# Two-block attention kernel: which steps stand beside which in the two attention stages

## What is computed

```
first block:  proj = norm(x) @ w_in
  8 heads of neighbourhood attention (qa, ka, va; mask and bias, head size 64)
  12 heads of dilated attention in 3 groups, dilation 1, 4, 16 (qb, kb rotated, vb)
  merged = gate_a * (o_a @ w_proj_a) + gate_b * (o_b @ w_proj_b);  x += gt1 * (merged @ w_o)
  x += gt2 * ffn(norm(x))
second block: joint attention over 512 tokens and 256 context tokens
  16 query heads in 8 pairs, 4 key heads; q, k normed per head, the 512 tokens' rotated
  x += gt1 * (o @ w_o);  x += gt2 * ffn(...), both for x and the context
  then a recurrent mixer in the place of attention, an ffn, and a last norm
```

## Time and profile before

| | us |
|---|---|
| median of 3 runs | 2740.07 |
| profiled execution | 2743.5 |
| its span, first to last instruction | 2741.7 |
| TensorE busy in the span | 2611.6 (95%) |
| VectorE, ScalarE, GpSimd busy | 1555.4, 1097.7, 1002.0 |

### The profile page before, as it was taken

How to read it: one execution, slowest core, us unless ns; L and a number is a source line. 1 busy time by engine, 2 the same in 40 slices (tenths; PEclk the granted TensorE clock), 3 DMA queues, 4 the chain that set the end, 5 groups by cost and what they waited for, 6 DMA issues and landing times. The chain is left out here.

```text
span 2741.7 us, 39030 instructions
## 1 busy us (share of the span) xinstructions
PE 2611.6 (95%) x15062; PEld 2181.7 (80%) x15062; DVE 1555.4 (57%) x2406; ACT 1097.7 (40%) x2040; POOL 1002.0 (37%) x571
## 2 busy tenths in 40 slices
PE   7997999999999999998999999999899998899998
PEld 5765778888888777777888888888788887788887
DVE  5554241787776256566755556655768777622224
ACT  4553442522324455556311211235555555522222
POOL 4344634556554312223332333341222112444444
PEclk9998999999999999999999999999999999999999
DMA  8643222354453100011333333411111111123222
GB/s 305 229 146 121 74 88 93 121 180 162 160 164 106 31 17 28 20 40 37 139 108 123 131 108 108 138 55 54 39 55 55 62 47 39 63 93 100 94 99 77
DMA packets 81463, 267.80 MB, mean 98 GB/s; under 512 B 8704, under 2 KB 16512, under 8 KB 81280
## 3 DMA queue, kind: packets, MB, share of 16 engines
q1 hardware_dynamic: 78944, 259.68, 28.2%
q10 hardware_dynamic: 2048, 4.33, 0.5%
q0 software_dynamic: 288, 1.31, 0.1%
HBM read 260.57 MB, written 4.72 MB: 97 GB/s over the span
## 5 line engine op out<-in xcount | busy, mean ns | idle before, releaser
L2261 POOL TENSOR_TENSOR SLO<-RAW,SHI 128x1024 fp32r<-128x1024 f32 (+1 forms) x290 | 716.5, 2473 | 1038.4 <-ACT SHI L2091 1038.4
L2091 ACT ACTIVATE SHI<-RAW 128x1024 fp32r<-128x1024 f32 (+1 forms) x334 | 345.1, 1037 | 949.6 <-PE PS L2526 947.8
L2524 PE MATMUL PS<-HLh,SHI 128*128 128x512 f32 (+1 forms) x1800 | 703.3, 391 | 7.6 <-DVE HLl L2330 4.7
L2526 PE MATMUL PS<-HLh,SLO 128*128 128x512 f32 (+1 forms) x1800 | 678.7, 377 | 0.0
L2525 PE MATMUL PS<-HLl,SHI 128*128 128x512 f32 (+1 forms) x1800 | 678.6, 377 | 0.0
L2524 PEld LDWEIGHTS PS<-HLh,SHI 128*128 128x128 f32 x1800 | 340.8, 189 | 79.8 <-issue 19.5
L2526 PEld LDWEIGHTS PS<-HLh,SLO 128*128 128x128 f32 x1800 | 340.2, 189 | 63.4
L2525 PEld LDWEIGHTS PS<-HLl,SHI 128*128 128x128 f32 x1800 | 341.1, 190 | 61.2 <-issue 6.3
L2524 PE MATMUL PS<-hh,SHI 128*128 128x512 f32 (+1 forms) x1024 | 363.1, 355 | 1.2 <-POOL hl L2280 1.2
L2526 PE MATMUL PS<-hh,SLO 128*128 128x512 f32 (+1 forms) x1024 | 356.4, 348 | 0.0
L2525 PE MATMUL PS<-hl,SHI 128*128 128x512 f32 (+1 forms) x1024 | 354.9, 347 | 0.0
(11 more groups left out here) (261 smaller groups left out, 3933.1 us busy)
## 6 DMA issues: line engine op xcount, KB each, us to landing
RAW<-in_k_w SPq DMA_DIRECT2D x318, 512.0 KB, 3.5
ADA<-in_k_w SPq DMA_DIRECT2D x132, 512.0 KB, 4.2
early<-in_k_w SPq DMA_DIRECT2D x12, 512.0 KB, 15.1
RAW<-in_k_w SPq DMA_DIRECT2D x16, 256.0 KB, 2.6
XL<-in_xT SPq DMA_DIRECT2D x4, 512.0 KB, 8.0
bi<-in_k_bias SPq DMA_DIRECT2D x16, 128.0 KB, 4.8
out<-XL SPq DMA_DIRECT2D x16, 128.0 KB, 1.8
bi<-in_k_bias SPq DMA_DIRECT2D x8, 192.0 KB, 3.9
```

The source lines that it names most:

```text
L2091: eng.activation(u.hi, u.w, ACT.Copy).then_inc(S["a_hi"], 1)
L2261: eng.tensor_tensor(u.lo, u.w, u.hi.bitcast(F32), ALU.subtract).then_inc(S["g_lo"], 1)
L2524: eng.matmul(st.out, lh, rh, start=st.first and j == 0, stop=False)
L2526: i = eng.matmul(st.out, ll, rh, start=False, stop=st.last and j == n - 1)
```

## The change

It has three edits.

1. `pipelined` has a switch, `shared`, that both stages set. A job without steps of its own no longer runs the tail before it; the tail is kept for the next job with steps. While a job waits, a "pause" is yielded ahead of each step of the tail, so that the attention sequence is asked for a step in between.
2. `weave` and `bgz` take "pause" as they take "wait".
3. Three empty pairs stand in `heads` between the 16 pairs of neighbourhood attention and the 8 dilated ones. A round whose pair is empty has no scores, flips or products for it.

```diff
@@ weave
-            known = len(emitted)
+            known, paused = len(emitted), False
             for p in sorted(left, key=lambda q: q[2]):
                 before = work[0]
                 got = next(p[0], "end")
-                if got == "wait":
+                if got in ("wait", "pause"):
                     p[3] = True
+                    paused |= got == "pause"
                     continue
@@ pipelined
-    def pipelined(jobs):
+    def pipelined(jobs, shared=False):
         tail = iter(())
         for job in jobs:
+            steps = 0
             while True:
...
                 if got == "wait":
+                    if shared:
+                        yield "pause"
                     yield next(tail, "wait")
                 else:
+                    steps += 1
                     next(tail, None)
                     yield
-            yield from tail
-            tail = new
+            if steps or not shared:
+                yield from tail
+                tail = new
         yield from tail
@@ attention
-            turn, read = 0 <= i - 2 < n, 0 <= i - 3 < n
+            turn, read = (0 <= k < n and pairs[k][0] is not None for k in (i - 2, i - 3))
...
-            if i < n:
+            if i < n and pairs[i][0] is not None:
@@ heads of the first stage
         heads += marked(na_items(j), [f"q {j}", f"k {j}"], f"na {j}")
+    heads += [None] * 6
@@ both weaves
-    weave((attention(heads, W, first_out), 0.6), (bgz(pipelined(dense)), 1.0))
+    weave((attention(heads, W, first_out), 0.6), (bgz(pipelined(dense, True)), 1.0))
-    weave((attention(heads, W, make2), 1.25), (pipelined(dense), 1.0))
+    weave((attention(heads, W, make2), 1.25), (pipelined(dense, True), 1.0))
```

More of the change, by code:

```diff
@@ L446, in weave @@
             else:
-                assert len(emitted) > known, "every sequence waits for another"
+                assert paused or len(emitted) > known, "every sequence waits for another"
     def run(gen):
```

## The result

The changed kernel takes 2753.04 us in the median of five runs (2751.29 to 2755.39). Beside it the kernel before took 2740.34 us (2739.62 to 2743.74). The ratio is 1.0045, 95% interval 1.0034 to 1.0056: slower by 12.7 us, where 15.5 less were forecast. The time lies outside the range as well.

The account below looks back on a forecast made before the run. PE was taken as the bound, busy 95% of the span, so time could come only from its idle time or clock. Terms -5.5 - 13.3 - 1.5 + 4.8 = -15.5 took 2740.07 to 2724.6 us, range 2711 to 2737.

Parts of the forecast that it names:

- the second stage, tiles 1 to 6: Query tiles' kept tails hold two PSUM banks during m0 to m2: +0.8 us a tile (-1.3 to +2.5), +4.8 in all.
- The walk through the banks: Second-stage tile, m0 to norms: new waits of 0.9, 0.3, 0.6 and 0.3, 2.1 us; 0.60 and 0.3 go.
- the low end of the range, 2711: Whole kernel: 2711 us, described as the sum with the best ends of passage and tiles.
- The third rival: m0 to m2 of six second-stage tiles: slower by PSUM banks, turning at 3.4 us more per tile, 2747 us; chance 0.13.
- First stage up to 217 us: Tails go beside the next job's chunks, removing norm waits of 0.69 and waits for VectorE: gain 5.5 us (4 to 5.8).
- The passage: Passage to dilated attention, 217 to 256 us: costs 8.5 instead of 21.8 us, a gain of 13.3 (9 to 19).
- The hole: First dilated scores wait for the rotated key from POOL, about 5.5 us (1.4 to 7), clock fall behind it 3.
- the second rival: Passage: Ada's VectorE step or a late unit delays the hole to 9 us, time 2733 or 2736; chance 0.12.
- The start of the second stage: First 30 us: the pause ends the rotation's wait, the second scores wait about 1.3 longer; gain 1.5 us (0 to 5).
- The forecast is wrong if the second stage changes its length by over 6 us: Sign in the profile after: a second-stage length change over 6 us would show the forecast wrong.

Follow-up runs that it names:

- e1: The changed kernel with the switch taken from the second stage, first stage as changed; 2726.7 us, ratio 0.9943 to the kernel before.
- e4: The changed kernel, but in the second stage both head norms run at once and only rotation and empty steps are kept; 2727.7 us, ratio 0.9948.
- e3: The changed kernel, but in the second stage VectorE copies a query tile's two PSUM banks to SBUF and the late norms read the copy; 2744.7 us.
- e11: The changed kernel, but second-stage query tiles' head norms run at once and only the giving back of their two banks stays late; 2741.6 us.

## Why the prediction was wrong

**The step that failed: the second stage, tiles 1 to 6.** It was priced at +0.8 us a tile, +4.8 in all, with +2.5 a tile as its upper end. The second norm of a tile comes every 44.2 us before and every 47.8 after (five periods each). These are the first and the last of the six, before and after:

```profile
987.41 0.67 PE L2532 MATMUL PS<-f,CONST 128*128 128x256 f32 x2 [0.83 <-ACT r L2118]
...
1208.47 0.67 PE L2532 MATMUL PS<-f,CONST 128*128 128x256 f32 x2 [0.60 <-DVE o L2388]
```

```profile
983.67 1.05 PE L2539 MATMUL PS<-f,CONST 128*128 128x256 f32 x2
...
1222.60 1.05 PE L2539 MATMUL PS<-f,CONST 128*128 128x256 f32 x2
```

That is (1222.60 - 983.67) - (1208.47 - 987.41) = 17.9 us in five periods, 3.6 a tile. The walk through the banks had the right order, and the two larger of its four waits came: m0's 0.9 as 0.7 for `o`, the norm's 0.6 as 0.58 for `XL`; the two of 0.3 did not, and all of the old 0.42 and 0.26 went. It stopped at the norms, where the banks come free. It left out m2's context chunk, whose bank is the flip's: 2.29 us in each of six tiles, for which the forecast has no term. But the step that moves is not only a holder of banks, it is also four instructions in three queues: a matmul, 0.69 + 0.63 us on ACT and 0.75 on VectorE. Before, it stood ahead of the reductions too, but early enough to be done in time; now VectorE's part ends 0.57 us too late for them, and the flip's copy is late by as much. On PE, the rotation and m0's context chunk no longer stand between the scores and the taker of that bank (3.73 us of work instead of 5.05). The walk counted the moved step's banks and not its places in the queues. Then the clock: the forecast let no wait of the second stage cost more than its own length, and three slow stretches came.

The sum of the walk was wrong as well. Waits of 2.1 come, and 0.6 and 0.3 go, which is +1.2 a tile and not +0.8; +0.8 takes the old 0.42 and 0.26 as gone altogether, which happened but was called unlikely. With +1.2 the forecast is 13.1 us less instead of 15.5. And the low end of the range, 2711, is not the sum with the best ends: 5.5 + 19 + 1.5 + 6 x 1.3 = 33.8 gives 2706. Neither changes the outcome.

**The third rival** had the place (m0 to m2 of six tiles), the size (3.4 us as its turn, 3.6 measured) and the sign, and 0.13 of the chance. Its mechanism was half of it: a queue on VectorE was called rare because VectorE is busy for 163 of 274 us. The share says nothing of one moment. The reductions that matter start just when the norm's step on VectorE ends (1027.35 behind 1026.68 + 0.75).

**First stage up to 217 us: -5.5.** Idle PE fell by 4.1 us. All five waits of 0.69 and the two for `qa` are gone, as said; some of it came back as a wait of 1.1 us for ACT at 180.77.

**The passage: -13.3.** The two marks leave 13.9 - 4.1 = 9.8. The bare tails and the chunkless rounds are gone and the first dilated scores came where they should. The hole is 7.05 us, not 5.5. The clock had not one but two slow stretches, from 234.5 to 242 us and from 251.5 to 255.5. Priced as in the forecast (busy 4.87 us at 0.54 and 3.95 at 0.57) they cost 3.9 us instead of 3. The second comes with a new wait of 1.57 us of a chunk for a flip's copy on ACT. The profile of `e1`, with the same first stage, has only the first stretch, and its mark stands at 344.9 us instead of 346.8. The tile's rotation in the profile after, on POOL and VectorE:

```profile
229.49 2.35 POOL L2268 TENSOR_TENSOR SLO<-RAW,SHI 128x1024 fp32r<-128x1024 f32 x1 [0.35 <-ACT SHI L2098]
229.84 3.07 DVE L2347 CUSTOM_DVE_ANT_0 ADA<-c,ADA,COL 128x1024 f32<-128x1024 f32 x1
231.80 2.24 POOL L2277 TENSOR_TENSOR f<-f,ROPE 128x512 f32<-128x512 f32 x1
...
232.85 2.27 DVE L2347 CUSTOM_DVE_ANT_0 ADA<-c,ADA,COL 128x1024 f32<-128x1024 f32 x1
234.18 2.90 POOL L2283 TENSOR_TENSOR qb<-f,r 128x512 f32<-128x512 f32 x1
...
237.13 2.93 PE L2551 MATMUL PS<-qb,qb 64*128 64x512 f32 x12 [7.05 <-POOL qb L2283]
```

SLO ahead of the rotation was foreseen. That two Adas on VectorE run beside it, and that POOL's steps are longer there, was a remark in the second rival and no term of the sum. From the rotation's matmul to the key it is 237.1 - 227.7 = 9.4 us instead of 7.8. Another tile of the same profile, with no Ada beside it, has the steps of the earlier trace rows:

```profile
296.07 2.38 POOL L2268 TENSOR_TENSOR SLO<-RAW,SHI 128x1024 fp32r<-128x1024 f32 x1
...
298.40 1.30 POOL L2277 TENSOR_TENSOR f<-f,ROPE 128x512 f32<-128x512 f32 x1
...
299.85 2.15 POOL L2283 TENSOR_TENSOR qb<-f,r 128x512 f32<-128x512 f32 x1
```

The product is 0.94 us shorter there and the sum 0.75, together about the 1.6 by which the hole was missed. That the Adas are the reason fits the rows, but no run changed only them.

**The start of the second stage: -1.5.** The second scores wait 2.95 instead of 1.46 us, 1.5 longer where 1.3 was foreseen. The rotation waits no more, as said, but the first head norm now waits 1.41 for a flip's bank, where the forecast had nothing:

```profile
926.30 0.70 PE L2551 MATMUL PS<-k,q 64*128 64x256 f32 x4 [2.95 <-ACT e L2133]
...
929.62 2.05 PE L2539 MATMUL PS<-f,CONST 128*128 128x512 f32 x2 [1.41 <-ACT pt L2139]
```

PE's idle time in the first 30 us went from 4.8 to 6.1 us. With the first tile the stage lost 21.6 - 17.9 = 3.7 us here and at its end instead of gaining.

**In all**: -13.9 instead of -18.8 in the first stage, +21.6 instead of +3.3 in the second. "The forecast is wrong if the second stage changes its length by over 6 us" was the sentence that decided.

## What to carry to other kernels

Moving a step later is moving all its instructions to new places in every queue: write down what then stands behind each of them, and follow that to the next buffer to come free. Do the same for the engine that was filled by the step: what it has left to do before it asks for that buffer is part of the wait. Where buffers are given in turn, the late one need not be the one that is held; here the longest wait was for a flip's bank, while a head norm's was held. The part of a tail that frees buffers is best run at once (`e4`). Keeping the rest, here the rotation, did no harm and gave nothing that the runs can tell.

## What the runs showed of the hardware

- TensorE's granted clock fell to 1.2 GHz for some 3.4 us around waits of 2.29 us in three of six tiles (changed kernel) and of 1.95 us in five of six (`e3`), with PE busy for over 90% of the stage. In `e11` waits of 1.3 us in every tile, and one of 2.63, brought no fall. So these rows show that waits of about 2 us can cost more than their length, and not which of them do.
- GpSimd's three steps of a rotation (SLO, product, sum) took 2.35, 2.24 and 2.90 us beside VectorE's Ada (two operands of 128x1024) and 2.38, 1.30 and 2.15 without one. The product and the sum each began while an Ada had 1.1 and 0.9 us still to run (229.84 + 3.07 - 231.80 and 232.85 + 2.27 - 234.18), about what they took longer (0.94 and 0.75). No run changed only this.
